# A chained two-block transformer layer: second input projection reordered around the decay chain, and a router that fixes the first expert of every block

## The reference

```python
u = rmsnorm(h, mix_norm); z = u @ w_in                       # 1024 -> 2000
q, k, v, r, a_low, q_lat, kv_lat, k_rope = split(z)          # 256,256,512,512,16,256,128,64
# gated linear attention (4 heads, chunks of 64)
log_a = log_sigmoid(a_low @ w_a2 + b_a) / 16;  b = cumsum of log_a inside a chunk
q_e = q*exp(b);  att = tril(q_e @ (k*exp(-b)).T);  upd = (k*exp(b_last-b)).T @ v
state_n+1 = exp(b_last)*state_n + upd;  o = att @ v + q_e @ state_n
y_gla = rmsnorm(o)*gain * silu(r)
# latent attention (4 heads): q from rmsnorm(q_lat) @ w_qb (128 plain + 64 rotary), k,v from rmsnorm(kv_lat) @ w_kvb
h = h + concat(y_gla, y_mla) @ w_out
# router: 1 of 8 groups, then 2 of its 8 experts; 64 experts of 1024->512->1024
t = rmsnorm(h, ffn_norm);  logits = t @ wg + bg, t @ we + be
# tokens are sorted by expert into blocks; each block: (silu(x@w_gate[e]) * (x@w_up[e])) @ w_down[e]
h = h + sum of the two experts' rows * gates;  out = rmsnorm(h, final_norm)
```

## Time and profile before

| what | value |
|---|---|
| median of 3 runs | 2826.2 us (2825.83 to 2826.87) |
| the profiled execution | 2825.43 us, of it the span 2823.6 us |
| PE busy | 2506.0 us (89%) |
| DVE busy | 1060.2 us (38%) |
| ACT busy | 465.8 us (16%) |
| read from HBM | 567.19 MB |

### The profile page before, as it was taken

How to read it: one execution, slowest core, us unless ns; L and a number is a source line. 1 busy time by engine, 2 the same in 40 slices (tenths; PEclk the granted TensorE clock), 3 DMA queues, 4 the chain that set the end, 5 groups by cost and what they waited for, 6 DMA issues and landing times. The chain is left out here.

```text
span 2823.6 us, 24528 instructions
## 1 busy us (share of the span) xinstructions
PE 2506.0 (89%) x9003; PEld 1163.0 (41%) x9003; DVE 1060.2 (38%) x1254; ACT 465.8 (16%) x732; POOL 179.7 (6%) x458
## 2 busy tenths in 40 slices
PE   8999999998998999999997897688888888888884
PEld 4444444466654444444445454333333333333331
DVE  3655530245553333310125634233333333333334
ACT  2000000255332000000102120011111111111111
POOL 0000000000000000000000000111111111111111
PEclk9999999998999999999996798899999999999997
DMA  7444543113001212322301000899999999999995
GB/s 272 149 149 147 178 136 100 45 45 105 1 1 60 88 61 87 93 59 73 106 30 35 1 16 28 361 417 415 413 415 406 412 408 413 403 411 409 412 402 218
DMA packets 182831, 563.19 MB, mean 199 GB/s; under 512 B 16864, under 2 KB 132848, under 8 KB 156544
## 3 DMA queue, kind: packets, MB, share of 16 engines
q1 hardware_dynamic: 172384, 554.10, 51.1%
q0 software_dynamic: 10400, 8.42, 1.0%
HBM read 567.19 MB, written 20.97 MB: 208 GB/s over the span
## 5 line engine op out<-in xcount | busy, mean ns | idle before, releaser
L1147 PE MATMUL ps<-slot,xT 128*64 128x512 f32 x2048 | 519.3, 666 | 156.2 <-DMA slot<-in_expert_w_up 154.5
L723 PE MATMUL ps<-hT,slot 128*128 128x512 f32 x1408 | 613.0, 596 | 13.0 <-ACT hT L1240 7.2
L723 PEld LDWEIGHTS ps<-hT,slot 128*128 128x128 f32 x1408 | 267.1, 191 | 350.3 <-issue 347.1
L1147 PEld LDWEIGHTS ps<-slot,xT 128*64 128x64 f32 x2048 | 156.5, 153 | 517.1 <-issue 308.2
L752 PE MATMUL ps<-big,slot 128*128 128x512 f32 x704 | 306.0, 594 | 3.4 <-issue 2.9
L1985 DVE COPY hT<-ps 128x256 f32<-128x256 f32 x64 | 27.2, 424 | 625.8 <-PE ps L1155 625.8
L1166 PE MATMUL ps<-slot,hT 128*64 128x512 f32 x1024 | 235.5, 602 | 1.2 <-DVE hT L1985 1.2
L1976 DVE RECIPROCAL xT<-xT 64x512 f32<-64x512 f32 x64 | 214.1, 3345 | 2.2
L752 PEld LDWEIGHTS ps<-big,slot 128*128 128x128 f32 x704 | 132.4, 190 | 176.2 <-issue 176.2
L1568 DVE RECIPROCAL eb<-eb 128x512 f32<-128x512 f32 x44 | 147.5, 3353 | 1.5
L1566 DVE TENSOR_SCALAR eb<-eb 128x512 f32<-128x512 f32 x44 | 18.8, 427 | 330.3 <-ACT eb L1250 330.3
(11 more groups left out here) (340 smaller groups left out, 2308.8 us busy)
## 6 DMA issues: line engine op xcount, KB each, us to landing
slot<-in_expert_w_gate SPq DMA_DIRECT2D x64, 2048.0 KB, 17.1
slot<-in_expert_w_up SPq DMA_DIRECT2D x64, 2048.0 KB, 22.4
slot<-in_expert_w_down SPq DMA_DIRECT2D x64, 2048.0 KB, 23.1
slot<-in_w_mod SPq DMA_DIRECT2D x18, 2048.0 KB, 7.8
slot<-in_w_gate SPq DMA_DIRECT2D x22, 1024.0 KB, 5.3
slot<-in_w_up SPq DMA_DIRECT2D x22, 1024.0 KB, 7.7
slot<-in_w_down SPq DMA_DIRECT2D x16, 1408.0 KB, 8.2
slot<-in_w_in SPq DMA_DIRECT2D x24, 512.0 KB, 5.9
```

The source lines that it names most:

```text
L723: last = mm(ps[:, 2 * j + g, :], w[:, g, k, j * P:(j + 1) * P], hT[:, k, META:TOK], start=(k == 0), stop=(k == KC - 1))
L1147: last = mm(ps[g * CAP:(g + 1) * CAP, j, :], xsT[j][:, k, :], w[g][:, k, :], start=(k == 0), stop=(k == KC - 1))
```

## The change

1. **Order of the projection.** The item with a_low, kv_lat, k_rope, q_lat goes first, then k, q, then r, then v. `w_a2` and `w_qb` go to slot 1, `w_kvb` alone to slot 2 when the first item is done. Units rotate over two pairs of banks (0 to 3); banks 4 to 7 serve the decay chain, which PE, ACT and DVE now run between the units. A unit waits for the copy of the unit two before it.
2. **Chunks, heads, latent units.** Chunk updates stand between the value units; the latent units stand between the gated heads. ACT takes the copies of the plain queries and keys. The barriers of phases 11, 12, 13, 16, 17, 18, 20 and 21 go.
3. **Router by tiles.** `u2` is turned, copied and multiplied tile by tile. Ranks and counts take 2 products instead of 14, from `Mh` and a running sum `Mc`.
4. **Fixed first experts.** Block n is expert n for n below 64 (also when it has no token); only rows beyond the first 64 of an expert go to further blocks. So the weights of experts 0 to 3 are issued without waiting for the router: all six slots, then gate and up of 2 and 3 as the slots come free.
5. **One-hot picking.** The rows of blocks 0 and 1 come not by a gather but by 32 products each of `u2` with a one-hot of the rank (`pick_rows`, `first_rows`). The tables come after the first gate and up product; the first gathers are for blocks 2 and 3.

The diff, cut to its core:

```diff
-        Sc = ring[0][:, 0:1056].rearrange("p (c t) -> p c t", c=2)
-        km = ring[0][:, 1056:2112].rearrange("p (c t) -> p c t", c=2)
+        km = ring[0][:, 0:1056].rearrange("p (c t) -> p c t", c=2)
...
+        qn = ring[2][:, 1024:3072].rearrange("p (h t) -> p h t", h=GH)
...
+        kn = [gk[:, 0], gk[:, 1], aL, part(9296, TOK)]
...
+        ITEM_SLOT = {3: 2, 0: 3, 2: 4, 1: 5}
...
+        UNITS = [(3, 0, 16, True, aL[0:16, :]), (3, 16 + 2 * P, P, True, kv), (3, 16 + 3 * P, ROPE, True, kr[0:ROPE, :]),
+                 (3, 16, P, False, ql[:, 0]), (3, 16 + P, P, False, ql[:, 1]),
+                 (0, 2 * P, P, True, gk[:, 0]), (0, 3 * P, P, True, gk[:, 1]), (0, 0, P, False, gq[:, 0]), (0, P, P, False, gq[:, 1]),
+                 (2, 0, P, False, gr[:, 0]), (2, P, P, False, gr[:, 1]), (2, 2 * P, P, False, gr[:, 2]), (2, 3 * P, P, False, gr[:, 3]),
...
-            b = 2 * (n % 4)
+            b = 2 * (n % 2)
...
+        JOINED = (14, 15, 19, 22)
...
+            for n in (3, 0, 2, 1):
+                c0, w = ITEMS2[n]
+                slot_n = ITEM_SLOT[n]
+                sp.wait_ge(freed[slot_n], u.take(slot_n, 1)[1])
+                sp.dma_start(w2(n), w_in2[:, :, c0:c0 + w]).then_inc(filled[slot_n], 16)
+                if n == 3:
+                    sp.wait_ge(freed[1], u.take(1, 2)[1])
+                    sp.dma_start(w_a2, a["gla_w_a2_2"][0]).then_inc(filled[1], 16)
+                    sp.dma_start(w_qb, a["mla_w_qb_2"][0].rearrange("(k p) n -> p k n", p=P)).then_inc(filled[1], 16)
...
+            sp.wait_ge(freed[2], u.take(2, 1)[1])
...
+            sp.wait_ge(freed[3], u.take(3, 3)[1])
...
+            first = [u.take(s, 1)[1] for s in range(N_SLOT)]
             sp.wait_ge(s_mo, GH * NT)
             sp.dma_start(gain_row, a["ffn_norm_2"].to_broadcast([P, D])).then_inc(s_row, 16)
+            for n in range(2):
+                sp.wait_ge(freed[n], first[n])
+                gate_or_up(0, n, 0)
+            sp.wait_ge(freed[2], first[2])
+            down_rows(0, 0)
             for t in range(NT):
                 sp.wait_ge(s_un, t + 1)
                 sp.dma_start(u_dram[t * P:(t + 1) * P, :], u2[:, t, :]).then_inc(s_ud, 16)
+            sp.wait_ge(freed[4], first[4])
+            gate_or_up(1, 1, 1)
+            sp.wait_ge(freed[5], first[5])
+            down_rows(1, 1)
+            sp.wait_ge(freed[3], first[3])
+            gate_or_up(1, 0, 1)
+            for n, done in enumerate((s_mg, s_mu)):
+                sp.wait_ge(done, 3)
+                gate_or_up(0, n, 2)
+            for n, done in enumerate((s_mg, s_mu)):
+                sp.wait_ge(done, 4)
+                gate_or_up(1, n, 3)
+            sp.wait_ge(s_my, 3)
+            down_rows(0, 2)
             sp.wait_ge(s_bet, 2)
+            n_pairs = sp.value_load(pairs_ix[0:1, 0:1], min_val=NE // 2, max_val=MAX_PAIRS)
...
+            with sp.Fori(2, n_pairs) as i:
...
+            unit(U_AL)
+            unit(U_KV)
+            decay_product()
+            unit(U_KR)
+            unit(U_QL)
+            unit(U_QL + 1)
+            unit(U_GK)
+            latent_sums()
+            unit(U_GK + 1)
+            unit(U_GQ)
+            unit(U_GQ + 1)
+            turn_keys()
+            for h in range(GH):
+                unit(U_GR + h)
+            unit(U_GV)
+            unit(U_GV + 1)
+            chunk_update(0)
+            unit(U_GV + 2)
+            chunk_update(1)
+            chunk_update(2)
+            unit(U_GV + 3)
+            chunk_update(3)
+            chunk_update(4)
+            unit(U_GV + 4)
+            pe.drain().then_inc(freed[ITEM_SLOT[1]], 1)
+            chunk_update(5)
+            chunk_update(6)
+            pe.wait_ge(s_kd, 2)
+            gla_scores(0)
+            chunk_update(7)
+            mla_unit(0)
+            mla_unit(1)
+            for h in range(GH):
+                gla_out(h)
                 if h + 1 < GH:
                     gla_scores(h + 1)
...
+                mla_unit(3 * h + 2)
+                gla_sum(h)
+                if h + 1 < GH:
+                    mla_unit(3 * h + 3)
+                    mla_unit(3 * h + 4)
...
+            turn_normed(0)
+            turn_normed(1)
+            logits(0)
+            turn_normed(2)
+            logits(1)
+            logits(2)
+            turn_normed(3)
+            logits(3).then_inc(s_lg, 1)
...
+            mm(ps[:, 1, 0:NT * NE], const("strict_t"), Mh.rearrange("p t e -> p (t e)"), start=True, stop=True, skip_group_check=True)
+            mm(ps[:, 1, NE:(NT + 1) * NE], ones, Mc.rearrange("p t e -> p (t e)"), start=False, stop=True,
+               skip_group_check=True).then_inc(s_rk, 1)
+            def first_rows(j):
+                for k in range(KC):
+                    for t in range(NT):
+                        last = mm(ps[:, 4 + j, k * CAP:(k + 1) * CAP], u2[:, t, :].rearrange("p (m k) -> p k m", k=KC)[:, k, :],
+                                  first_hot[j][:, t, :], start=(t == 0), stop=(t == NT - 1))
+                last.then_inc(s_xt, 1)
+            pe.wait_ge(s_pos, 1)
+            first_rows(0)
...
-            pe.wait_ge(s_gat[0], 16)
-            turn_rows(0)
-            gate_up(0, 1, 0, 16)
-            turn_rows(1)
+            gate_up(0, 1, 0, None)
+            pe.wait_ge(s_pos, 2)
+            for w in range(2):
+                for n in range(2 * NT):
+                    last = mm(ps[0:CAP, 2 + w, 0:TAB], slot_hot[w][:, n, :], block_hot[:, n, :], start=(n == 0), stop=(n == 2 * NT - 1))
+            last.then_inc(s_tb, 1)
+            pe.wait_ge(s_pos, 3)
+            first_rows(1)
+            pe.wait_ge(s_bet, 1)
+            n_more = pe.value_load(pairs_ix[0:1, 1:2], min_val=NE // 2 - 1, max_val=MAX_PAIRS - 1)
...
+            unit_copy(U_AL)
+            unit_copy(U_KV)
             act.wait_ge(s_dt, 1)
...
+            unit_copy(U_QL)
             act.wait_ge(s_S, 1)
...
+            unit_copy(U_QL + 1)
+            act.wait_ge(*unit_out(U_QL + 1))
+            av(gq, ql, ACT.Square)
+            av(tmp[:, 0, :], kv, ACT.Square).then_inc(s_lq, 1)
+            act.wait_ge(s_lss, 1)
+            av(tmp[:, 1, 0:SEQ], ps[:, 4, :], ACT.Sqrt, scale=1.0 / 256, bias=eps_col[:, 0:1])
+            av(halves(tmp[:, 0, :]), ps[:, 6:8, 0:264], ACT.Sqrt, scale=1.0 / P, bias=eps_col[:, 0:1]).then_inc(s_lstd, 1)
+            unit_copy(U_GQ)
+            unit_copy(U_GQ + 1)
             act.wait_ge(s_kt, 1)
...
+            for pair in range(2):
+                unit_copy(U_GR + 2 * pair + 1)
+                gate_pair_exp(pair)
+            for t in range(5):
...
+                mla_unit_copy(3 * h)
                 act.wait_ge(s_go, h + 1)
                 av(osq, ps[:, 1 + 2 * (h % 2), :], ACT.Square).then_inc(s_gsq, 1)
+                mla_unit_copy(3 * h + 2)
...
+            for n in range(N_CHUNK - 1):
+                state(n)
+            gla_mask(0)
+            state(N_CHUNK - 1)
             for h in range(GH):
...
+                rope_queries(h)
+                if h + 1 < GH:
+                    gla_mask(h + 1)
+                gla_head(h)
...
+            v.tensor_tensor(Mc[:, 0, :], Mk[0][:, 0, :], Mk[1][:, 0, :], ALU.add)
+            link(v.tensor_tensor(Mh, Mk[0], Mk[1], ALU.add))
+            for t in range(1, NT):
+                last = v.tensor_tensor(Mc[:, t, :], Mc[:, t - 1, :], Mh[:, t, :], ALU.add)
...
+            def pick_rows(j):
+                link(v.tensor_tensor(first_hot[j], rank[:, :, j:j + 1].to_broadcast([P, NT, CAP]),
+                                     const("iota_cap").unsqueeze(1).to_broadcast([P, NT, CAP]), ALU.is_equal))
+                v.tensor_tensor(first_hot[j], first_hot[j], Mh[:, :, j:j + 1].to_broadcast([P, NT, CAP]), ALU.mult).then_inc(s_pos, 1)
+            pick_rows(0)
...
-            gather(0, 0, 2)
-            gather(1, 1, 3)
+            pool.wait_ge(s_pos, 4)
+            pool.wait_ge(s_bet, 2)
+            n_more = pool.value_load(pairs_ix[0:1, 1:2], min_val=2, max_val=MAX_PAIRS - 1)
+            gather(0, 2, 2)
+            gather(1, 3, 3)
```

More of the change, by code:

```diff
@@ L968, in _, with decay_product @@
-            pe.wait_ge(s_ktc, 1)
-            for n in range(N_CHUNK):
+            def decay_product():
+                pe.wait_ge(filled[1], u.take(1, 2)[0] + 32)
+                pe.wait_ge(*unit_out(U_AL))
+                for p in range(2):
+                    for g in range(2):
+                        last = mm(ps[:, 4 + 2 * p + g, 0:264], w_a2[:, p * P:(p + 1) * P], aL[0:16, g * 264:(g + 1) * 264],
+                                  start=True, stop=True)
+                last.then_inc(s_la, 1)
@@ L1096, in _ @@
[L1096 to L1106 removed]
+                return last
```

467 lines of the change are left out of this document (225 added, 242 removed).

## The result

Four runs of each: median 2791.05 us after (2781.86 to 2792.07) against 2826.01 before (2824.76 to 2826.87), ratio 0.9868 (95% interval 0.9856 to 0.988). The forecast was 2758.7 with a range of 2745 to 2778: the sign was right, the gain was half of the one forecast (35.0 of 67.5 us), and the time lies outside the range. The profiled execution took 2792.07 us, its span is 2790.2.

The account below looks back on a forecast made before the run. Bound: PE and DVE time ahead of the experts, then DMA engines streaming weights from 1797.3. Gains of 44.4 (projection to heads) and 23.1 us (router and stream) make 67.5: 2826.2 - 67.5 = 2758.7 us, range 2745 to 2778.

Parts of the forecast that it names:

- Part 1: Projection, decay chain and heads: work interleaved on PE, attention begins at 1561.3 against 1605.7, gain 44.4 us.
- 2.3 us of interlock: Heads: 2.3 us added because 9.1 us of DVE work in each head interlocks with PE's 10 us.
- 3.2 of late states: State chain before the heads: last three states and a mask on DVE end some 3.2 us behind PE.
- Rivals A and D: A: heads stay a lower-clock relay, 2780, chance 0.16. D: clock swings through projection and heads, up to 2944, chance 0.03.
- rival C: Projection to heads without waits, one-hot products at 0.115 us: 5.5 + 4 us more gain, 2749, chance 0.08.
- Rival E: Expert blocks: experts without tokens add blocks, slower from 5 empty ones (78.7 us); chance 0.01.
- The attention "stays as it is": Attention stage: its 60.8 us unchanged, as is the output projection behind it.
- 64 cost 7.4 to 14.3 us ... I take 10.6 for the first and 8.2 for the second: One-hot row picking of blocks 0 and 1: 64 records each, 7.4 to 14.3 us; 10.6 and 8.2 taken.
- part 2: Router and first two blocks: logits 5.7 us sooner, gate and up of block 1 done at 1789.7 in old times.
- The period afterwards is unchanged: Expert weight stream: same bytes and products, so still 15.73 us a block.
- the two [barriers] at the very end are under 1 us: End of the kernel: removing the last two barriers is worth under 1 us, left out of the sum.
- Part 3: Weight stream: continuous from 1789.8 instead of 1797.25, 184 transfers left instead of 187; gain 7.4 + 15.7 = 23.1 us.
- Rival B: Blocks 0 to 3: PE falls behind, early weight transfers gain nothing; 15.7 us less gain, 2774.4, chance 0.10.

Follow-up runs that it names:

- edit 2: Changed kernel with gate and up weights of experts 0 and 1 reordered so one-hot products read neighbouring columns of u2: 2777.24 us median.
- experiments 9 to 11: Changed kernel, separately: no POOL drain at the last join, 2771.67 to 2782.43 us; eight early POOL drains added, 2780.48 to 2793.26; one indirect transfer more, 2773.34 to 2784.67.
- experiment 7: Changed kernel with the first six expert weight transfers issued only after the router has named the experts: 2781.0 us median.
- edits 2 and 6: Changed kernel, separately: one-hot products reading neighbouring columns, 2777.24 us median; block 1 gathered by POOL instead of picked by one-hot products, 2771.7 us median.
- the first trace: Profiled execution of the changed kernel, no further edit, from its first four runs: 2792.07 us, span 2790.2.
- the second: Trace of the changed kernel run once more, unaltered: 2781.14 us, span 2779.2; median of its five runs 2781.77.
- edits 2 and 9: Changed kernel with one-hot products reading neighbouring columns and POOL counted in at the last join without a drain: together 2761.41 us median.
- experiments 2, 4 and 14: Changed kernel with one-hot products reading neighbouring columns: alone, 2777.24 us; plus nine constant products filling PE's wait, 2767.98; plus no POOL drain at the last join, 2761.41.
- experiment 5: Changed kernel with three products of constants on PE behind the first two groups of attention scores: 2783.93 us median.

## Why the prediction was half right

**Part 1 held.** Forecast 190.7 us from the first unit to the attention, measured 186.2 and 187.3, at clock 0.99 and 0.98. Where 2.3 us of interlock and 3.2 of late states were added, PE waited 1.5 and 1.2 us in its latent query units (behind the states and the rotated queries on DVE). Rivals A and D are out: no unit waited for the copy of the unit two before it long enough to show. The 3.3 to 4.5 us by which it is better are most of rival C's first 5.5. Rival E is out too: every trace has 64 gate transfers. (The prediction counted the first dip of the clock line as slices 22 to 24 and the second as 26; they are 22, 23 and 25, 26. Its stages come from the rows by windows, so nothing rests on it.) Behind rival D stood a rule of the Trainium skill ("TensorE: Matmul & The Clock Gate", "A second HAM failure mode: psum-queue depth-cycling"); by 0.99 over 186 us, on two pairs of banks, the trace does not agree with it here.

**The attention "stays as it is": half wrong.** It is 61 to 64 us or 71 by execution. One trace of before showed 62.6 from its first product to that of the output projection, and nothing in one trace could have told the second form. No part of the range held it.

**The step that failed first: "64 cost 7.4 to 14.3 us ... I take 10.6 for the first and 8.2 for the second".** They took 15.5 and 15.5, above the upper bound. The prediction named the nearest rows, and among them the row turning "whose weights are read with the same stride", at 0.144 us a record; but those are transpositions of 64 rows, one record each, and the other two rows have no stride. So it is not the stride alone: a strided transposition of 64 rows takes 0.13 us, little over the 0.115 of a plain full-clock record, while in products of 128 rows, two records each, the stride doubles the full-clock time. Whether the rows or the kind of operation makes that difference was not separated. The bound from the unstrided records at the lower clock was taken for the worst case, when the one thing that set this operation apart had no row. That is 12.2 us of the miss; some 4.2 more are gate and up, on the clock that was low behind the strided products (9.4 and 9.1 against 7.1 each), and the tables and copies between take half a microsecond less than forecast. Together 15.7 to 15.9, the table's first constant stretch; edit 2 gives 12.6 of it back. The prediction named two signs of a mis-sized part 2, a group over 15 us and a first gather landing after 1743; both came (15.5, and the gather issued only at 1748.0). By the Trainium skill ("TensorE: Matmul & The Clock Gate", section "LDWEIGHTS (loading the stationary operand)"), a load costs its columns over 1.2 in ns, by which an estimate for 128 columns is 107 ns: the plain records, 0.115 us each at the full clock, come near it; at clock 0.50 (0.217) and with the stride (0.242) they do not.

**The step that failed second: the tail, behind "The period afterwards is unchanged".** The period is unchanged: 1020.3 us from the fourth gate transfer to the end, less the gap of 10.05 us (10.75 less 0.70), is 1010.2, against 1010.6 forecast (1026.35 less 15.7). What was put at nothing is the tail: "the two [barriers] at the very end are under 1 us" was said of the barriers that go, and no term stood for the one that stays. The change took POOL from 130 indirect transfers to 128, and so, by experiments 9 to 11, its drain from 0.70 to 10.75 us.

**Part 3: right sum, wrong owner.** The three transfers fewer (15.7 us) are there, as the last paragraph's sum shows. But they are no merit of the early issue: PE's work ahead of the fourth gate transfer is long enough to cover six transfers issued after the router (experiment 7). With that work shortened, as by edits 2 and 6, the late issue was not tried. Rival B asked this question at the wrong place: it expected the loss in blocks 0 to 3, with the gain forfeited.

Account of the first trace: 5.0 (chance ahead) - 4.5 (part 1 better) + 8.7 (attention, chance) - 0.6 (to the one-hots) + 15.9 + 9.6 = 34.1. Of the second: 0.8 - 3.3 + 0.2 - 0.9 + 15.7 + 10.6 = 23.1. Both are whole. Without the two terms called chance, the miss is 20 to 22 us, and edits 2 and 9, priced at 22.6 together, win it back: 2761.4 against the forecast 2758.7. That this comes so near is in part luck, since part 1 was 3 to 4 us better than forecast.

## What to carry to other kernels

Where a new operation has no row, ask in which property it differs from the nearest ones (here a stride of 8 in the stationary operand) and let the bounds rest on that property, not on the clock. Follow a changed count (of transfers, waits, instructions) to the end of the program, and read the last 50 us of the changed trace as closely as the changed stage. When the trace before shows a stage with a stretch at the lower clock, take a second trace before calling the stage fixed; and before crediting an early start, check what would have covered the late one.

## What the runs showed of the hardware

- A stationary operand of 128x128 f32 read at every eighth column: 0.24 us a record with 64 moving columns, at granted clock 0.50 and, in the 14 records of the second group that had it, at 1.00; with neighbouring columns 0.217 and 0.115. Transpositions of 64 rows with the same stride: 0.13 (1.05 us for 8).
- The granted clock can fall while PE has no idle time: under the second strided group, from 1.00 to 0.50 at 1747.8, 3.3 us after its start, with PE busy since 1732.8 (first trace); the same 3.2 to 3.4 us after its start in all eight traces that have such a group, and not under the second plain group of experiments 2, 4 and 14. What of their activity does it, no run here shows.
- POOL: with 128 indirect transfers behind it a drain took 10.75 us (10.52 where it came last and off the path), in all nine kernels with that number; with 129 or 130 the 129th was issued 3.0 us late and the drain took 0.70 (0.47 where it came last), in all five. What becomes due at that count is not shown, nor what smaller counts do.
- The attention stage takes 61 to 64 us or 71 us by execution, by where the clock stands at 0.50 and for how long. In the changed kernel and its variants the long form goes with a stretch at 0.50 near 809 us (ten traces of ten; none of the three short ones has it; experiment 5 is the exception). What decides it is open.
